# Attention heads taken in pairs: scores on the two row halves of the TensorE array, values on the two column halves

## The reference, cut to what matters

```python
D_MODEL, SEQ, HEAD_DIM, N_Q_HEADS, N_KV_HEADS, GQA_GROUP = 1024, 256, 64, 16, 4, 4
WINDOW = 128

def windowed_gqa_sink(x, w_qkv, w_o, sink):
    qkv = x @ w_qkv                        # 16 query heads, 4 key heads, 4 value heads
    ...                                    # rotary turn on the first 16 of 64 features of q and k
    s = einsum(q, k) * HEAD_DIM ** -0.5    # per head; 4 query heads share a key head
    s = where(|qpos - kpos| <= WINDOW, s, -inf)
    m = maximum(max(s, axis=-1), sink)
    p = exp(s - m)
    probs = p / (sum(p, axis=-1) + exp(sink - m))
    o = einsum(probs, v)
    return o @ w_o
```

## Time and profile before

| | us |
|---|---|
| median of three timed executions | 1621.99 |
| the profiled execution | 1618.47 |
| its span, first to last instruction | 1617.2 |
| TensorE busy with products | 1200.2 (74%) |
| VectorE busy | 466.0 (29%) |
| ScalarE busy | 302.7 (19%) |
| share of the chain that ended last: DMA | 50% |
| share of that chain: TensorE | 34% |

### The profile page before, as it was taken

One profiled execution on the slowest core, in us unless ns is written; L12 is line 12 of the kernel. 1 busy time (PEld: TensorE's weight loads), 2 busy tenths in 40 slices (PEclk: granted clock), 3 DMA queues, 4 the chain that ended last, 5 costly groups with the idle time before them and its releaser, 6 DMA issues.

```text
span 1617.2 us, 18970 instructions
## 1 busy us (share of the span) xinstructions
PE 1200.2 (74%) x8305; PEld 660.6 (41%) x8305; DVE 466.0 (29%) x980; ACT 302.7 (19%) x602; POOL 62.7 (4%) x88
## 2 busy tenths in 40 slices
PE   7998856578576656998776565656655799989987
PEld 6655411145122112885531111111111588545883
DVE  5435301200220000747420000100100567554524
ACT  4430101000310000373110000000000154340520
POOL 2000100000000000021000000000000100001000
PEclk9899978889797777999897778887788899999999
DMA  9704999999999999544999999999999722106410
GB/s 358 279 1 165 421 425 427 424 419 415 426 424 428 425 424 414 192 147 168 404 423 426 423 427 427 423 427 425 424 427 424 275 85 105 52 14 235 146 53 26
DMA packets 89667, 503.32 MB, mean 311 GB/s; under 512 B 6915, under 2 KB 15569, under 8 KB 56817
## 3 DMA queue, kind: packets, MB, share of 16 engines
q1 hardware_dynamic: 84224, 492.78, 74.6%
q10 hardware_dynamic: 3680, 8.04, 1.4%
q0 software_dynamic: 1680, 1.30, 0.2%
HBM read 501.00 MB, written 1.10 MB: 310 GB/s over the span
## 4 chain that ended last, share of the span: by engine, by line
DMA 50%; PE 34%; DVE 8%; ACT 5%; issue 1%; POOL 1%; SPq 1%; ACTq 0%; DVEq 0%
DMA weight_ring<-in_moe_w_gate_up 28%; DMA weight_ring<-in_moe_w_down 17%; PE bank L411 5%; PE bank L1252 4%; PE bank L323 3%; PE bank L324 3%; PE bank L325 3%; DMA weight_spare<-in_ada_w 3%; PE bank L1279 3%; DMA weight_ring<-in_even_w_in 2%; DVE weight_ring_rounded L363 1%; PE bank L2226 1%; PE bank L826 1%; PE bank L648 1%; PE bank L632 1%
## 5 line engine op out<-in xcount | busy, mean ns | idle before, releaser
L1252 PE MATMUL bank<-weight_ring,expert_tokens 128*32 128x512 f32 x2048 | 321.3, 762 | 206.7 <-DMA weight_ring<-in_moe_w_gate_up 200.8
L1252 PEld LDWEIGHTS bank<-weight_ring,expert_tokens 128*32 128x32 f32 x2048 | 66.2, 125 | 434.3 <-DMA weight_ring<-in_moe_w_gate_up 256.6
L1279 PE MATMUL bank<-weight_ring,actT 128*32 128x256 f32 x2048 | 165.3, 481 | 77.4 <-DMA weight_ring<-in_moe_w_down 66.8
L1373 DVE TENSOR_TENSOR act<-silu,bank 128x256 f32<-128x256 f32 x32 | 13.4, 420 | 436.7 <-ACT silu L1423 436.7
L1279 PEld LDWEIGHTS bank<-weight_ring,actT 128*32 128x32 f32 x2048 | 75.3, 133 | 155.8 <-DMA weight_ring<-in_moe_w_down 68.0
L1378 DVE COPY expert_outs<-bank 32x256 f32<-32x256 f32 x64 | 26.8, 418 | 265.4 <-PE bank L1279 264.4
L1423 ACT ACTIVATE silu<-bank 128x256 f32<-128x256 f32 x32 | 12.3, 384 | 483.7 <-PE bank L1252 483.7
L363 DVE TENSOR_TENSOR weight_ring_rounded<-weight_ring,weight_ring_rounded 128x1024 fp32r<-128x1024 f32 (+1 forms) x64 | 73.4, 1210 | 28.2 <-ACT weight_ring_rounded L347 28.1
L347 ACT CAST weight_ring_rounded<-weight_ring 128x1024 fp32r<-128x1024 f32 (+1 forms) x68 | 65.8, 1046 | 20.4 <-DMA weight_ring<-in_lru_w_in 12.8
L1432 ACT COPY expert_outs<-bank 32x256 f32<-32x256 f32 x64 | 23.3, 365 | 232.6 <-PE bank L1279 231.8
L448 POOL TENSOR_TENSOR norm_rstd<-norm_var,minus_half 128x1 f32<-128x1 f32 x12 | 18.3, 1526 | 953.2 <-DVE norm_var L436 953.2
(11 more groups left out here) (444 smaller groups left out, 1859.5 us busy)
## 6 DMA issues: line engine op xcount, KB each, us to landing
weight_ring<-in_moe_w_gate_up SPq DMA_DIRECT2D x128, 2048.0 KB, 31.0
weight_ring<-in_moe_w_down SPq DMA_DIRECT2D x64, 2048.0 KB, 31.1
weight_ring<-in_ada_w SPq DMA_DIRECT2D x8, 2048.0 KB, 15.7
weight_ring<-in_even_w_in SPq DMA_DIRECT2D x5, 2048.0 KB, 15.3
weight_ring<-in_odd_w_in SPq DMA_DIRECT2D x5, 2048.0 KB, 8.1
weight_spare<-in_ada_w SPq DMA_DIRECT2D x4, 2048.0 KB, 19.5
weight_ring<-in_lru_w_in SPq DMA_DIRECT2D x4, 2048.0 KB, 24.0
weight_ring<-in_attn_w_qkv SPq DMA_DIRECT2D x2, 2048.0 KB, 15.4
```

The lines of the kernel that those rows point to most:

```text
L1252: last = pe.matmul(up[CAP * j:CAP * (j + 1), :], B.xs[:, t, e * CAP:(e + 1) * CAP], w[:, t % 2, :, j, :], start=(t == 0), stop=(t == T - 1))
L1279: last = pe.matmul(K[3][CAP * q:CAP * (q + 1), 0:QC], B.actT[i][:, s, j * CAP:(j + 1) * CAP], w[:, jj, s, q, :], start=(j == 0 and s == 0) ...
```

## The change

Heads are taken in pairs: head `g` of the lower and of the upper key head of a group of eight (rows 0 to 63 and 64 to 127 of the turned queries and keys). The head loops run over 8 pairs and three more rounds.

- Scores: the two heads' products alternate, one on rows 0 to 63, one on rows 64 to 127 of the array, each into its own bank. Four banks (two pairs) are used instead of two.
- Values: the two heads' products alternate, one on columns 0 to 63, one on 64 to 127.
- Small steps (sum, reciprocal, bound, sink) run once for a pair, on four elements instead of two. The four diagonal matrices come from one step with two tensors, both broadcast, instead of two steps per head with a scalar. The sink is added to the bound by a new VectorE step, and the sink's exponential reads its result.
- The maxima, the exponentials and the copies out of PSUM stay one or two for each head as before.
- The order of heads in `B.o` is another, so `o0` and `o1` are loaded in four parts of 64 partitions each.
- The first half of the output product is begun in the loop: feature tiles 0 and 1 in round 8, 2 and 3 in round 9, ahead of the values of those rounds. The output uses banks 0 to 3 instead of 6, 7, 4 and 5.
- Buffers: three pairs of exponentials and two pairs of turned probabilities; the third and the second lie in the place of the queries, which are no longer needed then.

The diff, cut to what the text speaks of:

```diff
+    def out_part_tensor(self, stage, banks, y, y_event, names, free, half, tiles):
...
+        for j in tiles:
             for c in range(2):
...
+                if c == 0:
                     pe.wait_ge(*sig.after(*y_event(j)))
                 last = pe.matmul(banks[2 * half + c], y[:, j, rows], w[c][:, j], start=(j == 0), stop=(j == T - 1))
...
+        if name[:-1] == "o":
+            rows = lambda m, i: d["attn_w_o"][0][(2 * m + i) * GROUP * HD:(2 * m + i + 1) * GROUP * HD, int(name[-1]) * 512:][:, 0:512]
+            return [(view(512)[64 * i:64 * i + 64, m * GROUP:(m + 1) * GROUP, :], rows(m, i).rearrange("(g d) n -> d g n", g=GROUP))
+                    for m in range(2) for i in range(2)]
...
+    SCORE_BANKS, PT_BANKS, O_BANKS = ((0, 1), (2, 3)), (4, 5), (6, 7)
+    OUT_BANKS = (0, 1, 2, 3)
...
-        for n in range(NQ + 3):
-            if n == 4:
+        for s in range(NPAIR + 3):
+            if s == 2:
                 pe.wait_ge(*sig.after("rotated", 1))
...
                 turned_queries(1)
...
+                elif s >= 2:
+                    pe.wait_ge(*sig.after("exp", s - 2))
                 for half in range(H):
+                    for i in range(2):
+                        r = slice(64 * i, 64 * i + 64)
+                        pe.matmul(banks[i][:, half * S:(half + 1) * S], B.qT[r, s, half * P:(half + 1) * P], B.kT[r, m, :],
+                                  start=(half == 0), stop=False, skip_group_check=True)
+                for i in range(2):
+                    pe.matmul(banks[i][:, P:P + S], B.ident_r, B.mask, start=False, stop=True, skip_group_check=True).then_inc(
+                        *sig.tell("scored", ("scores", s, i)))
+            if 2 <= s < NPAIR + 2:
+                p = s - 2
+                pe.wait_ge(*sig.after("scales", p))
...
+            if s in (NPAIR, NPAIR + 1):
+                self.out_part_tensor(*out, 0, range(2 * (s - NPAIR), 2 * (s - NPAIR) + 2))
+            if s >= 3:
+                p = s - 3
...
                 for kk in range(H):
+                    for i in range(2):
+                        last = pe.matmul(bank[64 * i:64 * i + 64, 0:S], vals[:, kk, (2 * m + i) * HD:(2 * m + i + 1) * HD],
+                                         B.pT[p % 2][i][:, kk, :], start=(kk == 0), stop=(kk == H - 1))
...
-                for half in range(H):
-                    v.tensor_scalar(B.scale[i % 2][:, half, :], B.ident, B.den[:, i, half:half + 1], None, ALU.mult).then_inc(
-                        *sig.tell("softmax_steps", ("scales", i)))
+                v.tensor_tensor(B.scale[p % 2], B.ident.unsqueeze(1).to_broadcast([P, 2 * H, P]),
+                                flat.unsqueeze(2).to_broadcast([P, 2 * H, P]), ALU.mult).then_inc(
+                    *sig.tell("softmax_steps", ("scales", p)))
...
+                for i in range(2):
+                    v.wait_ge(*sig.after("scores", p, i))
+                    v.tensor_reduce(B.neg_max[:, 2 * p + i, :], K[self.SCORE_BANKS[p % 2][i]].rearrange("p (h k) -> p h k", h=H), AX.X,
+                                    ALU.max, negate=True).then_inc(*sig.tell("softmax_steps"))
...
+                v.scalar_tensor_tensor(B.neg_max[:, two, :], B.neg_max[:, two, :], HD ** -0.5, sinks(B.neg_sink), ALU.mult, ALU.min).then_inc(
+                    *sig.tell("softmax_steps", ("neg_max", p)))
+                v.wait_ge(*sig.now("softmax_steps"))
+                v.tensor_tensor(B.at_sink[:, two, :], B.neg_max[:, two, :], sinks(B.sink), ALU.add).then_inc(
+                    *sig.tell("softmax_steps", ("below_sink", p)))
...
+                for i in range(2):
+                    for half in range(H):
+                        a.activation(B.sm[p % 3][i][:, half, :], K[self.SCORE_BANKS[p % 2][i]][:, half * S:(half + 1) * S], ACT.Exp,
+                                     scale=HD ** -0.5, bias=B.neg_max[:, 2 * p + i, half:half + 1],
+                                     accum_out=B.total[:, 2 * p + i, half:half + 1]).then_inc(*sig.tell("exponentials"))
+                a.wait_ge(*sig.after("below_sink", p))
+                a.activation(B.at_sink[:, two, :], B.at_sink[:, two, :], ACT.Exp).then_inc(*sig.tell("exponentials", ("exp", p)))
```

More of the change, by code:

```diff
@@ L396, in split_x_vector @@
                 *sig.tell("x_split", ("features", stage, pair)))
[L398 removed]
+    def out_part_tensor(self, stage, banks, y, y_event, names, free, half, tiles):
         sig, pe = self.sig, self.pe
         w = [self.plain(name).rearrange("p (t c) -> p t c", t=T) for name in names]
[L402 to L403 removed]
+        rows = slice(half * P, (half + 1) * P)
+        for j in tiles:
             for c in range(2):
[L405 to L409, removed]
+                if j == 0:
+                    if free[2 * half + c] is not None:
+                        pe.wait_ge(*sig.after(*free[2 * half + c]))
+                    pe.wait_ge(*sig.after("arrived", names[c]))
+                if c == 0:
                     pe.wait_ge(*sig.after(*y_event(j)))
@@ L413, in out_product_tensor @@
                     last.then_inc(*sig.tell("out_product", ("out_product", stage, half, c), ("free", names[c])))
+    def out_product_tensor(self, stage, banks, y, y_event, names, free, begun=0):
+        sig, pe = self.sig, self.pe
+        self.out_part_tensor(stage, banks, y, y_event, names, free, 0, range(begun, T))
+        w = [self.plain(name).rearrange("p (t c) -> p t c", t=T) for name in names]
+        for c in range(2):
+            if free[2 + c] is not None:
+                pe.wait_ge(*sig.after(*free[2 + c]))
+            for j in range(T):
+                last = pe.matmul(banks[2 + c], y[:, j, P:2 * P], w[c][:, j], start=(j == 0), stop=(j == T - 1))
+            last.then_inc(*sig.tell("out_product", ("out_product", stage, 1, c), ("free", names[c])))
     def norm_rows_scalar(self, stage):
@@ L622, in attention_tensor @@
                 turned_queries(1)
[L623 to L626, removed]
+            if s < NPAIR:
+                m, banks = s // GROUP, [K[b] for b in self.SCORE_BANKS[s % 2]]
+                pe.wait_ge(*sig.after("qT", s // 2))
                 pe.wait_ge(*sig.after("kT"))
-                if n >= 2:
-                    pe.wait_ge(*sig.after("exp", n - 2))
-                r = slice(64 * i, 64 * i + 64)
-                for half in range(H):
[L632 to L644, removed]
-                for kk in range(H):
[L646 to L664, removed]
```

118 lines of the change are left out of this document (68 added, 50 removed).

## The result

| | before | after |
|---|---|---|
| median of the timed executions, us | 1622.01 (4: 1617.31 to 1623.99) | 1602.38 (4: 1596.62 to 1604.02) |
| span of the profiled execution, us | 1617.2 | 1602.5 |
| first score to end of the output product, us | 91.15 | 70.83 |

The ratio of the times is 0.9877, with a 95% interval from 0.9844 to 0.9910: 19.6 us between the medians, 1.2%, clearly more than the 0.3% that a measurement of this kernel can tell. The predicted time was 1603 with a range from 1597 to 1611.

What follows compares the result with a forecast made beforehand. TensorE bound the attention loop, whose end set the weight stream behind it. Eight pairs at 4.90 us plus start and tail ended at 122.4 instead of 140.25, winning 17.8 us: 1603 us, range 1597 to 1611.

Steps and rivals of the forecast that it cites:

- The stage behind moves with the attention: Behind the attention: each microsecond won before 140.25, the output product's end, should move all that follows by one.
- rival 5: Behind the attention: stream not set by attention's end, or gain given back waiting for slots; 1618 to 1622 us; chance 4%.
- The halves work at once: Attention loop on TensorE: a pair's two heads overlap, scores taking 1.06 us and values 1.01 us together.
- Rival 2: Attention loop on TensorE: neither row nor column halves overlap; 5.97 us a pair, 1613 us in all; chance 7%.
- Rival 1: Scores in the attention loop: row halves don't overlap; 5.12 us a pair, 1606.5 us in all; chance 15%.
- The ring: Attention loop: VectorE and ScalarE steps from scale to scale set the pace, 4.90 us a pair, longer than TensorE's 4.27.
- TensorE's own pair: Attention loop: TensorE's scores 1.06, masks 0.31 + 0.11, turning 1.78 and values 1.01 make 4.27 us a pair.
- The start: Loop's beginning: scores begin at 49.18, scale 2 at 66.2; 64.5 without a clock fall, 68.1 with one as long as before.
- rival 3: Loop's beginning and scale step: clock doesn't fall at 53.28 and scale takes 0.5 us; 1600 us in all; chance 8%.
- The tail: Loop's end: from scale 6 at 85.8 through last turnings, values and output passes to the output product's end at 122.4.
- The time: Whole kernel: 17.8 us won, 1600.7 from the profiled execution, 1604.2 from the runs' median; 1603 us said.
- Rival 4: Attention loop: clock falls and stays low because TensorE idles in each pair; 7.9 us a pair, 1634 us; chance 4%.

Runs made afterwards that it cites:

- output tiles ahead: Changed kernel with one output-product feature tile ahead of each of the last two turnings, instead of two tiles behind them: stretch 67.85 us, median 1597.09 us.
- all three moves: Changed kernel with maxima one round ahead, values' copy one round later, one output tile ahead of each last two turnings: pair 4.30, stretch 65.80, median 1591.74 us.

## Why the prediction was right, point by point

- **The stage behind moves with the attention.** Right. Over the thirteen traces taken after the prediction the time from the end of the output product to the end of the program lies between 1474.1 and 1481.3 us, and the kernel with the longest stretch (1479.5) and that with the shortest (1478.2) both lie between these. This scatter of 7 us, in stages that no kernel touched, is what the totals carry. The first expert stage alone shows it more sharply: its last product ends 501.7 to 504.5 us behind the output product in all fourteen traces, and at 625.6 where it was 642.9, 17.3 us earlier. The sign of rival 5 was less than 17.
- **The halves work at once.** Right for both: 1.06 us from a pair's scores to its masks (74.16 to 75.22) and 1.01 for its values (87.51 in the chain with the output tiles ahead), forecast 1.06 and 1.01. Rivals 1 and 2 fall. Rival 2, priced at 5.97 a pair, came to 6.74 in TensorE's old order. Rival 1, priced at 5.12 a pair, was measured at 5.54; what ended the overlap there also brought a second change of shape and its mask out of the shadow of the first.
- **The ring.** Right in kind, 4.90 forecast and 4.67 measured. The misses are small and on one side: bound to first exponential 0.20 for 0.27, the sink's exponential to the sum 0.26 for 0.33, the two maxima 1.32 for 1.37. Scale to maxima was 0.61 for 0.65. What failed is the word *the*: I wrote that the copy of the values ends just as the exponentials do, "slack 0.1", and costed it at nothing. It belongs to a ring of its own. The steps of the prediction's tail give 0.34 + 0.46 + 0.7 + 1.9 + 1.0 = 4.4 for it, 0.5 shorter than the ring it took; measured it is 4.68, since scale to turning takes 0.75, turning 1.98 and values to copy 1.14, and the other ring came out at 4.67. So the term at nothing cost nothing in the pair here, but it hid that cutting the first ring would gain nothing.
- **TensorE's own pair.** 4.27 forecast, 4.30 measured in the kernel with both rings cut.
- **The start.** First score to scale 2: 17.0 us forecast with a fall of the clock, 14.95 measured without; the prediction's own value without a fall was 15.3. That is rival 3's first half, and the larger part (2.1) of the 2.4 us by which the stretch was shorter than forecast (73.2 forecast, 70.83 measured).
- **The tail.** 36.6 us from scale 6 to the end forecast, 37.0 measured. The line of steps held, the delays by the early passes included. Its last sentence counts 16 passes, 6.9 us, as done by the end of the last values, beside values that end 10.8 us earlier. That is the same sum told in two parts, and not a gain by the early passes: without them the last values end 6.7 us earlier still and the stretch is the same. They are worth nothing where they stand.
- **The time.** 17.8 us forecast, 20.3 measured in the stretch, 19.6 between the medians. The prediction's 1603 had been set between two base times that differ by 3.5 us; that it agrees with 1602.38 to 0.6 us is luck. The start was 2.1 us shorter than forecast (1.7 of them because the clock did not fall), four pairs 0.7 shorter, the tail 0.4 longer, and by the median of the kernel before alone the forecast would have been 1604.2. That it lies in the range is not luck: the errors are small ones, of known terms.
- **The clock stays up in the loop.** Rival 4 did not come. Over 65.3 to 84.2 TensorE was at work in 16.91 of 18.90 us with a granted clock of 1.00.
- The Trainium skill, "TensorEngine Tiling (Array Packing)", section "Performance Considerations", warns that packing does not speed up the emptying of PSUM. The trace agrees in its result: after packing, two rings through VectorE's and ScalarE's steps set the 4.67 us. What bound here was not the amount of their work, though, as VectorE idled over 1 us a pair and the same work in another order let the pair fall to 4.30, but its order.

What stays open: why the clock falls at about 54 us in some traces and not in others, and how much of the gain between the medians is that fall; where the 7.3 us come from that the kernel with TensorE's old order has; and whether the time behind the attention grew a little. It was 1476.9 and 1474.1 in two traces with the old kernel and 1478.9 on average in the twelve others, but the one among these whose attention ends as late as the old one has 1479.5.

## What to carry to other kernels

When a bound is lifted, add up every closed ring of waits through two engines, not each engine's busy time, and write them side by side: two rings of equal length hide each other. Here each single cut left the pair at 4.67, and only both together paid. Work moved "into a wait" pays only if it stands ahead of the instruction that waits; behind it, it delays whoever waits for the next step. To end the overlap on TensorE in these experiments, exchanging the order wasn't enough; a product on the full array between the two heads did it. And before two stretches are compared, look whether the granted clock was the same in both.

## What the runs showed of the hardware that was not expected

- Two heads' products on different row halves (or column halves) overlap even if all of one head's are issued before the other's: eight passes of 256 columns in 1.14 us in either order, where four passes of one head alone take 1.13 us. The engine did not hold the second head's products back behind the first head's.
- A step on 512 elements with two tensors, both inputs broadcast, takes 0.69 us on VectorE, as one without a broadcast does that reads one input from PSUM. From its start to the next step it is 0.61 (74.72 to 75.33); two steps of half that size in all, with a per-row scalar, took 0.39 (75.20 to 75.59), so four would take 0.78, an estimate.
- From the last score pass (64 rows of the array) to the first mask product (128 rows) TensorE's weight load stands idle 0.33 us in the row at 75.22 of the new loop, and from the last value pass (64 columns) to the next scores 0.39 us in the kernel with all three moves, where no other wait hides it: 0.72 us a pair. With TensorE head by head there are two of each in a pair. Part of what pairs save are such changes; whether the shape makes the pause is not shown by itself, as the mask products also have another type (fp32r).
- After a wait of 1.00 us the granted clock fell to 0.50 in both traces of the kernel before; after one of 1.53 us at the same place it stayed at 1.00 in the kernel after.
